# Inner normalisations of a hybrid decoder step: where the low parts of the new activations are made, and fewer throwaway products

## The chip, the cores and the metric

One core of one Trainium2 chip runs the whole program. The metric is the device time of one execution in microseconds (us); lower is better. Beside it there is one profiled execution with a trace of every engine: TensorE (PE, and PEld for its weight loads), VectorE (DVE), ScalarE (ACT), GpSimd (POOL) and the queue that loads weights (SP).

## The reference

One inference step of a two-layer decoder trunk for 288 token rows: 256 of a new sequence and 32 of eight running ones. Around each of the two mixers (first RWKV-7 beside retention, then gated DeltaNet) stand two SwiGLU networks. Every one of these six parts is followed by a normalisation:

```python
def layer_norm(x, g, b):
    xf = x.astype(jnp.float32)
    xc = xf - jnp.mean(xf, -1, keepdims=True)
    var = jnp.mean(xc * xc, -1, keepdims=True)
    return xc * lax.rsqrt(var + LN_EPS) * g + b
...
def trunk(x, pos0, states, p):
...
    for l in range(DEPTH):
        i = l // 2
        f = swiglu(h, p['ffn_w_gate'][l, 0], p['ffn_w_up'][l, 0], p['ffn_w_down'][l, 0])
        h = layer_norm(DEEPNORM_ALPHA * h + 0.5 * f, p['ln_g'][l, 0], p['ln_b'][l, 0])
...
        h = layer_norm(DEEPNORM_ALPHA * h + m, p['ln_g'][l, 1], p['ln_b'][l, 1])
        f = swiglu(h, p['ffn_w_gate'][l, 1], p['ffn_w_up'][l, 1], p['ffn_w_down'][l, 1])
        h = layer_norm(DEEPNORM_ALPHA * h + 0.5 * f, p['ln_g'][l, 2], p['ln_b'][l, 2])
```

All is computed in single precision.

## The kernel before, in words

**Layout.** The activations lie transposed: 1024 channels are eight tiles (d = 0 to 7) of 128 rows by 288 tokens. `r3` holds the residual sum, `x` the activations. For TensorE each operand is split in a high part, which a short format holds exactly, and the low part that is left: `xhi` and `xlo` for the activations, `whi` and `wlo` for the weights. A product is three matmuls in a row, high by high (L2265), high by low weight (L2266) and low by high weight (L2269).

**Weights** come in units of 128 output channels. In the stages that follow a normalisation a unit has eight tiles of 128x128, so 24 matmuls. SP loads the units into four buffers. ACT makes the high part of a unit (`split_hi`, L2223), DVE the low part (`split_lo`, L2228), each into one of two buffers; a unit is split as soon as the unit two before it has been used. On ACT and DVE the order of the work is written out: in an `up` stage they first deal with the result of the unit that is done (ACT the gate function, L2347; DVE the product with the gate, L2438) and then split the unit two ahead.

**Phases** run in the order ffn0, norm0, ab0, norm1, ffn1, norm2, ffn2, norm3, gdn0, norm4, ffn3, norm5. The first five normalisations are the inner ones. norm0 is followed by the stage `za` (whose ACT and DVE code is in `ab_scalar` and `ab_vector`), norm1, norm2 and norm4 by an `up` stage, norm3 by the one-unit stage `ba` and then `qk` of the DeltaNet mixer.

**A normalisation** is spread over four engines, each with its own function `norm` (on POOL `sum_tiles`):

- POOL adds the first seven tiles of `r3` while the stage before ends (L2524).
- PE multiplies that sum and the last tile with a matrix of 1/1024, which gives the mean (L2291, L2293); later the eight squares in the same way, which gives the variance (L2298). Then come `WARM` = 16 throwaway products into a bank that nobody reads (`keep_warm`, L2285; single precision, so each is two matmul records). Then the stage that follows begins; its first unit waits before each matmul for the tile of `xhi` or `xlo` that it reads (L2264, L2268).
- DVE subtracts the mean (L2462), splits a unit of weights, takes the reciprocal (L2471), and scales eight tiles of `r3` in place (L2473, semaphore `scaled`). After all eight it makes eight low parts: tile plus bias minus `xhi` (L2479, semaphore `x_lo`, one for even and one for odd tiles).
- ACT squares (L2365), splits a unit of weights, takes the root (L2370), and after each scaling makes a high part: tile plus bias, rounded (L2376, semaphore `x_hi`). After all eight it makes the eight whole tiles of `x` in full precision (L2381, semaphore `x_new`), which the next residual sum reads. It then loads the function table of the next stage (L2354 in an `up` stage, L1678 in `ba`).

At that time both units of weights that fit in the buffers are already split, so the third unit of the stage is the first to be split after the normalisation.

**POOL after a normalisation.** In norm0 it goes on at once to `ab_pool`: it issues a transfer of old rows (L1323), clears a column, and copies the rows into place (L1326, semaphore `shift_pad`), for which ACT waits before the first rows of `za`. After norm1 it issues the transfer of constants for the DeltaNet mixer. After norm3 it goes to `gdn_pool`: a transfer (L2088), and a copy (L2091, semaphore `conv_pad`), for which DVE waits after the stage `ba`, ahead of its short operations on the decay rows (from L1882). In the `up` stages it splits the hidden activations.

The helper `low_parts` (L390 to L393) makes low parts on DVE and POOL elsewhere, at the input and at the end of both mixers, by a plain subtraction.

Of the kernel before, what the change touches and what calls it, by code (L numbers as in the profile page):

```python
# [23 lines left out]
DT = D // P  # L24
# [37 lines left out]
WARM = 16  # L62
# [235 lines left out]
def delta_kernel(nc, a):  # L298

    ctx = ExitStack()  # L300
    with ctx:
# [2015 lines left out]
        def _(act):  # L2317
# [38 lines left out]
            def norm(n):  # L2356
# [9 lines left out]
                if second_unit(n):  # L2366
# [4 lines left out]
                                     bias=eps).then_inc(drained[bank_of(("var", n))], 1)  # L2371
                for d in range(DT):
                    act.wait_ge(sem("scaled"), DT * n + d + 1)
                    b = pc("ln_b", n * DT + d)
                    if f"norm{n}" != phases[-1]:
                        nc.scalar.activation(xhi[:, d, :], r3[:, d, :], ACT.Identity, bias=b).then_inc(x_hi, 1)  # L2376
                    else:
                        nc.scalar.activation(x[:, d, :], r3[:, d, :], ACT.Identity, bias=b).then_inc(sem("x_new"), 1)
                if f"norm{n}" != phases[-1]:
                    for d in range(DT):  # L2380
                        nc.scalar.activation(x[:, d, :], r3[:, d, :], ACT.Identity, bias=pc("ln_b", n * DT + d)  # L2381
                                             ).then_inc(sem("x_new"), 1)
# [25 lines left out]
        def _(dve):  # L2408
# [47 lines left out]
            def norm(n, stage_name):  # L2456
# [14 lines left out]
                link(nc.vector.reciprocal(m(T, T), m(0, T)))  # L2471
                for d in range(DT):
                    nc.vector.scalar_tensor_tensor(out=r3[:, d, :], in0=r3[:, d, :], scalar=pc("ln_g", n * DT + d),  # L2473
                                                   in1=m(T, T), op0=ALU.mult, op1=ALU.mult
                                                   ).then_inc(sem("scaled"), 1)
                if f"norm{n}" != phases[-1]:
                    for d in range(DT):
                        dve.wait_ge(x_hi, DT * X_VERSION[n] + d + 1)
                        nc.vector.scalar_tensor_tensor(out=xlo[:, d, :], in0=r3[:, d, :],  # L2479
                                                       scalar=pc("ln_b", n * DT + d),  # L2480
                                                       in1=xhi[:, d, :].bitcast(F32), op0=ALU.add,
                                                       op1=ALU.subtract).then_inc(x_lo[d % 2], 1)
# [23 lines left out]
        def _(pool):  # L2506
# [9 lines left out]
            def sum_tiles(n):  # L2516
# [10 lines left out]
                ins.then_inc(sem("summed"), 1)  # L2527

# [152 lines left out]
```

## Time and profile before

| what | us |
|---|---|
| median of three runs | 1718.11 |
| lowest and highest of them | 1716.66, 1719.91 |
| span of the profiled execution, first to last instruction | 1714.2 |
| PE busy in it | 1592.8 |
| DVE, ACT, POOL busy in it | 890.9, 644.6, 407.2 |
| mean granted clock of TensorE in it | 0.944 of full |

The span is the profiled execution's own time on the engines; no other time is listed for that execution, and the runs' times are taken around the program as a whole. A row of a timeline gives the start, the duration, the engine, the line, the operation, what it writes and reads, how many like it follow without a break (x8), and in brackets the idle time of the engine before it and what ended that. A matmul's duration includes its way through the array, so that records overlap; its cost in a stream is the step to the next start.

### The profile page before, as it was taken

To read this page: it belongs to the slowest core of one execution; us is meant where nothing else is said; L and a number is where in the kernel's file an instruction comes from. 1 tells how busy PE (TensorE), PEld (TensorE's weight loads), DVE (VectorE), ACT (ScalarE), POOL (GpSimd) and SP (SyncE) were. 2 spreads that over 40 slices of the span, in tenths; PEclk is the share of its full clock that TensorE was granted. 3 is DMA by queue.
4 is the path that set the end of the run, shared out by engine and by line. 5 is a ranking of instruction groups with operands and counts; after the bars stand their busy time and mean duration, and the time that the engine had idled before them with its cause. 6 is when DMAs were issued, how large, how long until landed. Compare 5 with 4: busy or idle time off the path is not lost.

```text
span 1714.2 us, 29766 instructions
## 1 busy us (share of the span) xinstructions
PE 1592.8 (93%) x11529; PEld 1498.7 (87%) x11529; DVE 890.9 (52%) x1235; ACT 644.6 (38%) x997; POOL 407.2 (24%) x442
## 2 busy tenths in 40 slices
PE   8999998798998799999999999898798987999997
PEld 7999987788788589999999999797785885899996
DVE  4444468754254364444544444786654734644444
ACT  4333365211032343333443333654634113533423
POOL 3332005324011322330023310000325413133200
PEclk9999999899599899999999999998998886999999
DMA  7555433000042145555345554242400201354551
GB/s 263 160 166 181 157 99 111 15 2 26 4 163 96 43 148 160 170 174 171 123 132 163 165 186 150 83 153 101 148 1 7 99 7 67 106 171 160 177 170 61
DMA packets 50614, 203.05 MB, mean 118 GB/s; under 512 B 5696, under 2 KB 5696, under 8 KB 49888
## 3 DMA queue, kind: packets, MB, share of 16 engines
q1 hardware_dynamic: 46224, 181.03, 32.1%
q0 software_dynamic: 4016, 19.61, 3.1%
q8 instruction: 63, 1.03, 0.2%
q10 hardware_dynamic: 288, 1.18, 0.2%
q14 instruction: 23, 0.19, 0.0%
HBM read 191.97 MB, written 9.83 MB: 118 GB/s over the span
## 4 chain that ended last, share of the span: by engine, by line
PE 81%; DVE 10%; ACT 4%; issue 3%; POOL 1%; DMA 0%; DVEq 0%; ACTq 0%; POOLq 0%
PE gemm L2265 20%; PE gemm L2269 19%; PE gemm L2266 19%; PE job L850 2%; PE gemm L2285 2%; DVE wlo L2228 2%; PE job L1551 2%; ACT whi L2223 1%; PE job L2298 1%; PE job L1662 1%; PE job L836 1%; PE job L1612 1%; PE job L1528 1%; PE job L662 1%; PE job L686 1%
## 5 line engine op out<-in xcount | busy, mean ns | idle before, releaser
L2228 DVE TENSOR_TENSOR wlo<-raw,whi 128x1024 fp32r<-128x1024 f32 (+1 forms) x319 | 424.0, 1329 | 468.4 <-ACT whi L2223 468.2
L2265 PE MATMUL gemm<-xhi,whi 128*128 128x288 f32 x2040 | 618.7, 303 | 29.4 <-DVE wlo L2228 19.4
L2269 PE MATMUL gemm<-xlo,whi 128*128 128x288 f32 x2040 | 606.9, 297 | 3.9 <-DVE xlo L392 3.8
L2266 PE MATMUL gemm<-xhi,wlo 128*128 128x288 f32 x2040 | 608.2, 298 | 0.0
L2223 ACT ACTIVATE whi<-raw 128x1024 fp32r<-128x1024 f32 (+1 forms) x319 | 358.0, 1122 | 486.7 <-PE gemm L2269 480.9
L2265 PEld LDWEIGHTS gemm<-xhi,whi 128*128 128x128 f32 x2040 | 389.0, 191 | 42.1 <-DVE wlo L2228 22.5
L2269 PEld LDWEIGHTS gemm<-xlo,whi 128*128 128x128 f32 x2040 | 390.2, 191 | 4.8 <-DVE xlo L392 4.1
L2266 PEld LDWEIGHTS gemm<-xhi,wlo 128*128 128x128 f32 x2040 | 389.6, 191 | 1.3
L2265 PE MATMUL gemm<-hhi,whi 128*128 128x288 f32 x704 | 208.5, 296 | 0.9 <-DVE wlo L2228 0.9
L2269 PE MATMUL gemm<-hlo,whi 128*128 128x288 f32 x704 | 208.7, 296 | 0.0
L2266 PE MATMUL gemm<-hhi,wlo 128*128 128x288 f32 x704 | 205.2, 292 | 0.0
L2537 POOL TENSOR_TENSOR hlo<-hb,hhi 128x288 f32 x88 | 140.3, 1595 | 14.4 <-POOL hhi L2535 14.4
L2535 POOL CAST hhi<-hb 128x288 f32 x88 | 37.4, 425 | 427.9 <-DVE hb L2438 427.9
L2266 PEld LDWEIGHTS gemm<-hhi,wlo 128*128 128x128 f32 x704 | 134.2, 191 | 0.0
L2265 PEld LDWEIGHTS gemm<-hhi,whi 128*128 128x128 f32 x704 | 132.2, 188 | 1.9 <-DVE wlo L2228 1.9
L2269 PEld LDWEIGHTS gemm<-hlo,whi 128*128 128x128 f32 x704 | 131.9, 187 | 0.0
L2347 ACT ACTIVATE sg<-gemm 128x288 f32<-128x288 f32 x88 | 36.2, 411 | 187.9 <-PE gemm L2269 187.9
L2438 DVE TENSOR_TENSOR hb<-sg,gemm 128x288 f32<-128x288 f32 x88 | 39.9, 454 | 54.1 <-PE gemm L2269 54.1
L2524 POOL TENSOR_TENSOR xsum<-xsum,r 128x288 f32<-128x288 f32 x30 | 26.0, 868 | 170.1 <-DVE r L2451 169.7
L1673 ACT ACTIVATE M<-job 128x512 f32<-128x512 f32 (+4 forms) x46 | 24.2, 530 | 105.3 <-PE job L1528 70.4
L2451 DVE SCALAR_TENSOR_TENSOR r<-x,gemm 128x288 f32 (+1 forms) x48 | 21.8, 454 | 75.3 <-PE gemm L2269 75.3
L861 ACT ACTIVATE M<-job 128x512 f32<-128x512 f32 (+6 forms) x44 | 18.6, 441 | 87.4 <-PE job L540 23.1
(405 smaller groups left out, 1781.8 us busy)
## 6 DMA issues: line engine op xcount, KB each, us to landing
raw<-in_w_dram SPq DMA_DIRECT2D x255, 512.0 KB, 3.3
raw<-in_w_dram SPq DMA_DIRECT2D x64, 704.0 KB, 4.0
s_space<-in_gdn_in_dram POOLq DMA_DIRECT2D x8, 512.0 KB, 6.3
out_gdn_s_dram<-s_space POOLq DMA_DIRECT2D x8, 512.0 KB, 3.0
M<-in_ret_in_dram POOLq DMA_DIRECT2D x1, 2048.0 KB, 9.1
out_ret_s_dram<-M POOLq DMA_DIRECT2D x1, 2048.0 KB, 8.1
x<-in_x_dram ACTq DMA_DIRECT2D x2, 576.0 KB, 6.5
out_y_dram<-x SPq DMA_DIRECT2D x2, 576.0 KB, 2.8
```

The costliest lines, as they stand in the source:

```text
L850: mm = pe.matmul(bank[:, h * P:(h + 1) * P], lhs[s][:, h, :], rhs[s][:, h, :], start=True, stop=True)
L1551: mm = pe.matmul(bank[:, h * P:(h + 1) * P], lhs[:, h, :], rhs[:, h, :], start=True, stop=True)
L2223: nc.scalar.activation(whi[c % SPL][:, 0:w], raw[c % RAW][:, 0:w], ACT.Copy).then_inc(hi_ready, 1)
L2228: nc.vector.tensor_tensor(wlo[c % SPL][:, 0:w], raw[c % RAW][:, 0:w], whi[c % SPL][:, 0:w].bitcast(F32), ALU.subtract).then_inc(lo_ready, 1)
L2265: pe.matmul(bank[:, 0:T], whi[s][:, w], hi[:, f0 + q, :], start=first, stop=False)
L2266: pe.matmul(bank[:, 0:T], wlo[s][:, w], hi[:, f0 + q, :], start=False, stop=False)
L2269: mm = pe.matmul(bank[:, 0:T], whi[s][:, w], lo[:, f0 + q, :], start=False, stop=last)
L2285: pe.matmul(gemm[0][:, 0:T], C("mean"), xsum[:], start=True, stop=True)
L2347: nc.scalar.activation(sg[:, j // 2, :], gemm[j][:, 0:T], ACT.Silu).then_inc(bank_free[j], 1)
L2438: nc.vector.tensor_tensor(hb[:, h, :], sg[:, h, :], gemm[j][:, 0:T], ALU.mult).then_inc(bank_free[j], 1)
L2535: nc.gpsimd.tensor_copy(hhi[:, f, :], hb[:, h, :]).then_inc(hid_hi, 1)
L2537: nc.gpsimd.tensor_tensor(hlo[:, f, :], hb[:, h, :], hhi[:, f, :].bitcast(F32), ALU.subtract).then_inc(hid_lo, 1)
```

## The change

Three edits, all at the five inner normalisations (the last one, whose result goes to the output, is left as it was).

1. On DVE the low part of tile d - 1 is made right after the scaling of each odd tile d, so that the order is: scale 0, scale 1, low 0, scale 2, scale 3, low 2, and so on. DVE makes no low parts of odd tiles.
2. ACT makes the whole tile of each odd d right after its high part, and the whole tiles of even d at the end. POOL makes the low part of each odd tile as the whole tile minus the high part, after its sum of tiles, waiting for `x_new`.
3. `WARM` is 10.

```diff
-WARM = 16
+WARM = 10
...
+                def whole(d):
+                    nc.scalar.activation(x[:, d, :], r3[:, d, :], ACT.Identity, bias=pc("ln_b", n * DT + d)
+                                         ).then_inc(sem("x_new"), 1)
+
                 for d in range(DT):
                     act.wait_ge(sem("scaled"), DT * n + d + 1)
-                    b = pc("ln_b", n * DT + d)
-                    if f"norm{n}" != phases[-1]:
-                        nc.scalar.activation(xhi[:, d, :], r3[:, d, :], ACT.Identity, bias=b).then_inc(x_hi, 1)
-                    else:
-                        nc.scalar.activation(x[:, d, :], r3[:, d, :], ACT.Identity, bias=b).then_inc(sem("x_new"), 1)
+                    if f"norm{n}" == phases[-1]:
+                        whole(d)
+                        continue
+                    nc.scalar.activation(xhi[:, d, :], r3[:, d, :], ACT.Identity, bias=pc("ln_b", n * DT + d)
+                                         ).then_inc(x_hi, 1)
+                    if d % 2 == 1:
+                        whole(d)
                 if f"norm{n}" != phases[-1]:
-                    for d in range(DT):
-                        nc.scalar.activation(x[:, d, :], r3[:, d, :], ACT.Identity, bias=pc("ln_b", n * DT + d)
-                                             ).then_inc(sem("x_new"), 1)
+                    for d in range(0, DT, 2):
+                        whole(d)
...
+                def low(d):
+                    dve.wait_ge(x_hi, DT * X_VERSION[n] + d + 1)
+                    nc.vector.scalar_tensor_tensor(out=xlo[:, d, :], in0=r3[:, d, :],
+                                                   scalar=pc("ln_b", n * DT + d),
+                                                   in1=xhi[:, d, :].bitcast(F32), op0=ALU.add,
+                                                   op1=ALU.subtract).then_inc(x_lo[0], 1)
+
                 for d in range(DT):
                     nc.vector.scalar_tensor_tensor(out=r3[:, d, :], in0=r3[:, d, :], scalar=pc("ln_g", n * DT + d),
                                                    in1=m(T, T), op0=ALU.mult, op1=ALU.mult
                                                    ).then_inc(sem("scaled"), 1)
-                if f"norm{n}" != phases[-1]:
-                    for d in range(DT):
-                        dve.wait_ge(x_hi, DT * X_VERSION[n] + d + 1)
-                        nc.vector.scalar_tensor_tensor(out=xlo[:, d, :], in0=r3[:, d, :],
-                                                       scalar=pc("ln_b", n * DT + d),
-                                                       in1=xhi[:, d, :].bitcast(F32), op0=ALU.add,
-                                                       op1=ALU.subtract).then_inc(x_lo[d % 2], 1)
+                    if d % 2 == 1 and f"norm{n}" != phases[-1]:
+                        low(d - 1)
...
                 ins.then_inc(sem("summed"), 1)
+                if f"norm{n}" != phases[-1]:
+                    for d in range(1, DT, 2):
+                        pool.wait_ge(sem("x_new"), DT * n + d // 2 + 1)
+                        nc.gpsimd.tensor_tensor(xlo[:, d, :], x[:, d, :], xhi[:, d, :].bitcast(F32), ALU.subtract
+                                                ).then_inc(x_lo[1], 1)
```

## Rows read from the trace of the kernel before

**Rows 1.** The page: the span, and the chain that ended last by engine.

```profile
span 1714.2 us, 29766 instructions
...
PE 81%; DVE 10%; ACT 4%; issue 3%; POOL 1%; DMA 0%; DVEq 0%; ACTq 0%; POOLq 0%
```

**Rows 2.** The timeline of DVE at norm1: start us, duration us, what.

```profile
628.25 3.52 DVE L2473 SCALAR_TENSOR_TENSOR r<-r,par,M 128x288 f32<-128x288 f32 x8
631.69 3.51 DVE L2479 SCALAR_TENSOR_TENSOR xlo<-r,par,xhi 128x288 fp32r<-128x288 f32 x8
638.55 1.22 DVE L2228 TENSOR_TENSOR wlo<-raw,whi 128x1024 fp32r<-128x1024 f32 x1 [3.35 <-ACT whi L2223]
```

**Rows 3.** The timeline of ACT at norm1.

```profile
628.80 3.54 ACT L2376 ACTIVATE xhi<-r,par 128x288 fp32r<-128x288 f32 x8 [2.57 <-DVE r L2473]
632.24 3.51 ACT L2381 ACTIVATE x<-r,par 128x288 f32<-128x288 f32 x8
635.77 1.28 ACT L2354 ACT_TABLE_LOAD   x1
...
637.46 1.05 ACT L2223 ACTIVATE whi<-raw 128x1024 fp32r<-128x1024 f32 x1
```

**Rows 4.** The timeline of PE at norm1: throwaway products, first unit, third unit.

```profile
625.52 7.92 PE L2285 MATMUL gemm<-xsum,cst 128*128 128x288 f32 x32
633.07 0.51 PE L2265 MATMUL gemm<-xhi,whi 128*128 128x288 f32 x1
633.42 0.29 PE L2266 MATMUL gemm<-xhi,wlo 128*128 128x288 f32 x1
...
639.83 0.40 PE L2265 MATMUL gemm<-xhi,whi 128*128 128x288 f32 x1
```

**Rows 5.** The timeline of ACT after norm0: the splits of two successive units.

```profile
240.45 1.06 ACT L2223 ACTIVATE whi<-raw 128x1024 fp32r<-128x1024 f32 x1 [0.97 <-PE gemm L2269]
...
243.65 1.06 ACT L2223 ACTIVATE whi<-raw 128x1024 fp32r<-128x1024 f32 x1 [1.78 <-PE gemm L2269]
```

**Rows 6.** The chain of waits after norm3, in order of time: start us, us, what.

```profile
1084.00 3.51 ACT x L2381 x8
...
1095.20 0.31 DVE mixc L1882
...
1099.36 0.40 PE gemm L2265
```

**Rows 7.** The view of line L392: ns shortest/median/longest, first and last start.

```profile
L392 POOL TENSOR_TENSOR xlo<-M,xhi x8: 792/1008/2439, 578.0 to 1447.4; 128x288 fp32r<-128x288 f32 x8
```

**Rows 8.** The timeline of POOL at the end of the first mixer.

```profile
578.01 0.88 POOL L392 TENSOR_TENSOR xlo<-M,xhi 128x288 fp32r<-128x288 f32 x1 [12.72 <-ACT xhi L995]
```

**Rows 9.** The timeline of DVE at the same time.

```profile
578.15 1.05 DVE L1286 SCALAR_TENSOR_TENSOR M<-M,par,r 128x288 f32<-128x288 f32 x1
```

**Rows 10.** The timeline of DVE at norm0.

```profile
231.97 3.53 DVE L2473 SCALAR_TENSOR_TENSOR r<-r,par,M 128x288 f32<-128x288 f32 x8
```

**Rows 11.** The timeline of POOL at norm0: the transfer and the copy after the sums.

```profile
215.45 0.57 POOL L1323 DMA_DIRECT2D M<-in_shift_in_dram  x1
...
217.52 0.39 POOL L1326 COPY M<-M 128x112 f32<-128x112 f32 x1 [1.36 <-DMA M<-in_shift_in_dram]
```

**Rows 12.** The timeline of POOL at norm3: the same two steps.

```profile
1071.85 0.57 POOL L2088 DMA_DIRECT2D M<-in_conv_in_dram  x1 [8.38 <-DVE r L2451]
...
1074.99 0.78 POOL L2091 COPY M<-M 128x576 f32<-128x576 f32 x1 [2.38 <-DMA M<-in_conv_in_dram]
```

**Rows 13.** Stretches: length, then PE, PEld, DVE, ACT, POOL busy; PEclk, DMA, GB/s.

```profile
369.50:372.90 3.40, 1.94 (x14) 1.62 (x14) 3.37 (x7) 0.00 (x0) 0.00 (x0) 1.00 0.00 0
372.90:376.30 3.40, 3.40 (x18) 3.40 (x18) 3.33 (x4) 0.77 (x2) 2.94 (x2) 0.51 0.00 0
...
495.80:499.20 3.40, 1.78 (x12) 1.32 (x10) 3.40 (x8) 1.06 (x1) 1.53 (x1) 1.00 0.90 371
499.20:502.60 3.40, 3.29 (x24) 3.29 (x25) 3.33 (x8) 0.00 (x0) 0.72 (x1) 1.00 0.52 174
```

## The prediction

> **What bounds the kernel now.** I read the page first, then the stretch around one inner normalisation on the three engines, then the chain of waits at the one normalisation that differs. The page shows TensorE on 81% of the chain that ended last, in a span of 1714.2 us [rows 1]. So an inner normalisation matters only through the moment at which PE can stream the weight units that follow it. The reader should see in norm1 that three engines work in rows: DVE scales eight tiles and then makes eight low parts [rows 2]; ACT makes eight high parts, then eight whole tiles, and only then loads the table for the next stage and splits the weights of the third unit [rows 3]; PE runs 16 throwaway products (32 records) from 625.52, starts the first unit at 633.07 and the third at 639.83 [rows 4].
>
> I count from the first scaling, 628.25 = 0. ACT ends its last whole tile at 632.24 + 3.51 = 635.75, which is 7.50. The third unit follows from that alone: table load, gate, high split (637.46 + 1.05), low split (638.55 + 1.22 = 639.77), PE at 639.83 [rows 2 to 4]. A unit of 24 products takes 3.20 us, the step between two high splits that each wait for one (240.45 to 243.65) [rows 5], so 0.133 us a product. The second unit therefore begins at 633.42 + 23 x 0.133 = 636.48 (8.23) and ends at 11.43; the third begins at 11.58, 0.15 us later, because ACT and DVE were the later ones [rows 4]. So **the tail of ACT, not the throwaway products, sets the third unit** after norm1, and norm2 and norm4 are followed by the same kind of stage. After norm3 the chain of waits runs through ACT's whole tiles (1084.00, 3.51 us) into DVE's short operations at 1095.20 and PE at 1099.36 [rows 6]: ACT again. Only after norm0 does PE's own first unit release ACT's next split (240.45, after 0.97 us idle for PE) [rows 5].
>
> **The change part by part.**
>
> *Six throwaway products fewer.* 7.92 us / 16 is about 0.49 us each [rows 4]; six are 2.9 us, so PE is free at about 2.1 instead of 4.8. It then waits for low parts, so this is worth nothing by itself; what covers it is the wait below.
>
> *The order of DVE and ACT.* The step from one scaling or high part to the next is 0.43 us ((631.69 - 628.25) / 8, and the same on ACT); one alone takes what eight in a row take less seven steps, 3.52 - 3.01 = 0.51 and on ACT 0.53 and 0.50, so 0.52; from DVE to ACT pass 0.04 (628.25 + 0.51 to 628.80) [rows 2, 3]. DVE now has four low parts in place of eight, which alone would end it 1.7 us sooner. But each low part stands between scalings and waits for a high part that waits for a scaling. A pair costs 0.51 + 0.04 + 0.52 + 0.04 + 0.43 = 1.54 us, where two scalings cost 0.86. The seventh scaling starts at 3 x 1.54 = 4.62, the eighth ends at 4.62 + 0.43 + 0.51 = 5.56, its high part starts at 5.60, and five whole tiles follow at steps of 0.43: the last ends at 5.60 + 5 x 0.43 + 0.52 = 8.27, or 8.28 with less rounding. ACT has the same sixteen operations as before, now with three stalls: **0.78 us later**, even if nothing else interferes.
>
> *Odd low parts on POOL.* Such a subtraction takes 0.79 us at the least and 2.44 at the most [rows 7]. While POOL held one (578.01, 0.88 us [rows 8]), the very form that DVE uses here, 128x288 with a per-partition scalar, took 1.05 instead of 0.51 us [rows 2, 9], so the later one waits for the other. In the new order POOL asks for tile 1 just after 1.94 (first whole tile), while DVE is at scaling 4 until 2.49; POOL then ends at about 3.14 and the low part of tile 2, ready at 2.65, ends at 3.45 instead of 3.17: +0.28. Tile 3 comes at about 3.57, falls into the fifth scaling, and holds the sixth until 4.85, which sets low part 4 back by 0.3. Tile 5 comes behind the eighth scaling, tile 7 when DVE is done (7.25 to 8.05). Sum +0.57: ACT ends at 8.85, **1.35 later than 7.50**. Bounds: 0.78 if POOL always finds a gap; if POOL gets in ahead of a scaling in each of the first pairs, two full delays of 0.54 and a little more, ACT ends at 9.5, +2.0. I take 1.35, since the row shows an operation already running to its end first.
>
> The Trainium skill states in "SBUF — State Buffer", section "SBUF: two separate sides", that a VectorE instruction with two SBUF inputs and a GpSimd one that reads SBUF exclude each other for the whole instruction, whichever starts first. By that rule every scaling and every low part counts, and the sum is the +5.4 below. The longest POOL row, 2.44 us, is longer than one instruction of waiting would make it; if POOL always waited so long for a pause of DVE, the sum would lie nearer to +2.6.
>
> *The first unit.* Its last product needs tile 7 from POOL at 8.05, so the second unit starts at about 8.25: as before (8.23). Bounds: 7.66 without the interference (-0.56), 8.87 with the worst (+0.65). I take 0. It counts at norm0 alone, since elsewhere ACT is later.
>
> *What POOL issues later.* The four subtractions stand ahead of what POOL did early. At norm0 the first scaling stands at 231.97 [rows 10], so POOL is done at 240.0. The shift transfer (215.45) and its copy 2.07 us later [rows 11] move to there, the copy to 242.1 to 242.5. ACT's first rows wait for that; its next split is due at 243.65 [rows 5], and 0.6 us of rows fit, so nothing; cover gone, each microsecond more of the transfer is one on PE. After norm3, whose first scaling is at 1084.00 - 3.99 = 1080.0 [rows 2, 3, 6], transfer and copy (1071.85 to 1075.77) [rows 12] move to about 1088 and 1092, before DVE needs them at 1095.20 [rows 6]: nothing. After norm1 the constants for a stage 450 us away: nothing.
>
> *Sum.* norm1, norm2, norm4: third unit +1.35 each. norm3: +1.35 through the chain of [rows 6]. norm0: 0. Together +5.4 us; bounds 4 x 0.78 - 0.56 = +2.6 and 4 x 2.0 + 0.65 = +8.7. The profiled execution's span is 1714.2; the median of the runs is 1718.11, 3.9 us more, and no other time of that execution is listed; I add the sum to the median, taking what lies around the span as unchanged. 1718.1 + 5.4 = **1723.5**, +0.31%.
>
> **The rivals.**
>
> *POOL and DVE don't get in each other's way* (not slower, by the measure below). The subtractions fall into DVE's three waits for high parts, about 0.25 us each. For: the gaps exist. Against: POOL needs 0.8 us, and the 1.05 us row. Only the order costs: 4 x 0.78 - 0.56 = +2.6, **1720.7**. It decides if no scaling in the changed trace takes over 0.6 us. Chance 0.20.
>
> *The low parts do set the units* (faster side). If the third unit's splits had room, each of five first units would end 0.56 sooner: -2.8, **1715.3**. It decides where ACT's last whole tile ends before 7.5, or its later work can slip. Against it, the 0.15 us by which ACT and DVE are already late at 639.83 [rows 2, 4]. Chance 0.10, half of it below the measure.
>
> *PE's clock falls.* With fewer throwaway products PE waits inside the first unit: between 4.6 and 8.0 it has some 12 products, 1.6 us of work. Elsewhere in the trace a stretch with 1.94 of 3.40 us busy was followed by 0.51, the lower level of 1.2 GHz, and one with 1.78 of 3.40 us was followed by 1.00 [rows 13], so either may come. Half clock for 3.4 us loses 1.7 us; after norm1, norm2 and norm4 the 1.4 us in which PE waits for the third unit take most of that, after norm0 nothing does. One such stretch at each adds 1.7 + 4 x 0.3 = 2.9 (at norm3 taken like the three); a second one at each is no longer covered and makes it 3.4 + 4 x 2.0 = 11.4. At the lower third of that, +5 on top of the forecast: **1728.5**. Chance 0.20.
>
> **How the numbers follow.** The forecast (1720.7 to 1726.8 by its bounds) has 0.50. A measurement of this kernel can tell about 0.2%, 3.4 us, from no change. Slower by more than that: forecast and clock, 0.70. Within: no interference 0.20 and half of the faster rival, 0.25. Faster: the other half, 0.05. The range takes in the forecast's bounds, the case without interference, and the nearer half of the clock's: 1719 to 1730; left out are the faster rival, 0.1, and the worse half of the clock's, 0.1. The forecast's own range is 1720.7 to 1726.8.
>
> **What would show it.** ACT's last whole tile should end 8.3 to 9.5 us after the first scaling (7.50 before); scalings or low parts of about 0.8 to 1.05 us beside POOL's subtractions; PE's third unit after norm1, norm2 and norm4 with about 1.3 us of idle before it, waiting for the low split; after norm3 PE's restart (1099.36) 1.35 us later against the scalings; after norm0 no change. The prediction is wrong if the third unit starts no later against the first scaling than 11.58, or if the granted clock drops behind a normalisation.

## The result, and the profile after

The changed kernel takes 1721.89 us in the median of 20 executions (1717.91 to 1734.28), the kernel before 1717.11 in 20 of the same series (1711.08 to 1722.06). The ratio is **1.0039, 95% interval 1.0025 to 1.0052**: slower by +4.8 us between the medians, where +5.4 was forecast. The ratio is not the quotient of the two medians (that is 1.0028); by the ratio the change costs 6.7 us (4.3 to 8.9). Five of the 20 lie above 1729, where none of the kernel before does (of its 109 executions in the later series one does, at 1731.12).

The page of the kernel after, its span and the chain that ended last, as in [rows 1]:

```profile
span 1717.8 us, 29646 instructions
...
PE 77%; DVE 12%; ACT 6%; issue 3%; POOL 1%; DMA 1%; DVEq 0%; ACTq 0%; POOLq 0%
```

PE has 4 points less of the chain than before, DVE and ACT have them. The timeline of DVE at norm1 of the kernel after (start us, duration us, what, and in brackets the idle time ahead with what ended it); the first scaling, 631.30, is 0, and [rows 2] are the same stretch before:

```profile
631.30 0.95 DVE L2485 SCALAR_TENSOR_TENSOR r<-r,par,M 128x288 f32<-128x288 f32 x2
632.42 0.52 DVE L2479 SCALAR_TENSOR_TENSOR xlo<-r,par,xhi 128x288 fp32r<-128x288 f32 x1 [0.18 <-ACT xhi L2381]
632.86 0.94 DVE L2485 SCALAR_TENSOR_TENSOR r<-r,par,M 128x288 f32<-128x288 f32 x2
633.98 0.80 DVE L2479 SCALAR_TENSOR_TENSOR xlo<-r,par,xhi 128x288 fp32r<-128x288 f32 x1 [0.17 <-ACT xhi L2381]
634.70 1.48 DVE L2485 SCALAR_TENSOR_TENSOR r<-r,par,M 128x288 f32<-128x288 f32 x2
636.11 0.51 DVE L2479 SCALAR_TENSOR_TENSOR xlo<-r,par,xhi 128x288 fp32r<-128x288 f32 x1
636.54 0.93 DVE L2485 SCALAR_TENSOR_TENSOR r<-r,par,M 128x288 f32<-128x288 f32 x2
637.64 0.80 DVE L2479 SCALAR_TENSOR_TENSOR xlo<-r,par,xhi 128x288 fp32r<-128x288 f32 x1 [0.17 <-ACT xhi L2381]
```

The timeline of POOL in the same stretch:

```profile
633.32 1.14 POOL L2538 TENSOR_TENSOR xlo<-x,xhi 128x288 fp32r<-128x288 f32 x1 [11.26 <-ACT x L2373]
634.88 1.00 POOL L2538 TENSOR_TENSOR xlo<-x,xhi 128x288 fp32r<-128x288 f32 x1 [0.41 <-ACT x L2373]
637.26 0.86 POOL L2538 TENSOR_TENSOR xlo<-x,xhi 128x288 fp32r<-128x288 f32 x1 [1.39 <-ACT x L2373]
638.54 0.81 POOL L2538 TENSOR_TENSOR xlo<-x,xhi 128x288 fp32r<-128x288 f32 x1 [0.42 <-ACT x L2373]
```

A low part takes 0.52 us when DVE is alone and 0.80 where it begins while POOL subtracts (633.98, inside 633.32 + 1.14). The pair of scalings at 634.70 takes 1.48 in place of 0.95: the sixth scaling alone takes 1.05, beside POOL's subtraction of tile 3. The timeline of ACT and then that of PE, which answer to [rows 3, 4]:

```profile
637.95 2.23 ACT L2373 ACTIVATE x<-r,par 128x288 f32<-128x288 f32 x5
640.19 1.28 ACT L2354 ACT_TABLE_LOAD   x1
...
641.89 2.21 ACT L2223 ACTIVATE whi<-raw 128x1024 fp32r<-128x1024 f32 x2
```

```profile
638.18 0.40 PE L2269 MATMUL gemm<-xlo,whi 128*128 128x288 f32 x1 [0.83 <-POOL xlo L2538]
...
639.64 0.29 PE L2265 MATMUL gemm<-xhi,whi 128*128 128x288 f32 x1
...
644.25 0.40 PE L2265 MATMUL gemm<-xhi,whi 128*128 128x288 f32 x1 [1.25 <-DVE wlo L2228]
```

ACT's last whole tile ends at 640.18, 8.87 after the first scaling (7.50 before). The second unit starts at 8.34 (8.23 before), the third at 12.95 (11.58 before), after 1.25 us in which PE waits for the low split. After norm2 and norm4 the same times come out within 0.02 us. After norm3 the chain of waits of the kernel after runs as in [rows 6]; from the first scaling (1085.84) to PE's restart it is 20.72 us, where it was 1099.36 - 1080.00 = 19.36:

```profile
1092.49 2.18 ACT x L2373 x5
...
1102.40 0.31 DVE mixc L1882
...
1106.56 0.40 PE gemm L2265
```

**Where the time is over the whole program** is read from stretches that run from the first scaling of one normalisation to that of the next. For the kernel after (length, busy time of PE, PEld, DVE, ACT and POOL, granted clock, DMA share, GB/s): first mixer, two SwiGLU stretches, second mixer, third SwiGLU stretch.

```profile
231.79:631.30 399.51, 352.28 (x2690) 312.65 (x2689) 219.76 (x350) 122.16 (x209) 109.58 (x108) 0.87 0.20 68
631.30:858.47 227.17, 222.64 (x1626) 218.25 (x1625) 105.30 (x111) 88.90 (x111) 53.23 (x55) 1.00 0.47 155
858.47:1085.84 227.37, 222.83 (x1626) 218.27 (x1625) 105.30 (x112) 88.89 (x111) 52.69 (x54) 1.00 0.47 152
1085.84:1483.36 397.52, 348.58 (x2307) 308.23 (x2306) 246.74 (x422) 168.64 (x343) 100.04 (x128) 0.88 0.23 79
1483.36:1710.53 227.17, 220.06 (x1614) 215.91 (x1612) 102.88 (x110) 86.90 (x109) 52.72 (x54) 1.00 0.43 140
```

The same view of the kernel before:

```profile
231.97:628.25 396.28, 350.12 (x2702) 311.74 (x2701) 219.89 (x355) 121.72 (x209) 105.75 (x101) 0.88 0.21 70
628.25:854.04 225.79, 224.20 (x1638) 220.37 (x1637) 106.07 (x115) 88.59 (x111) 48.83 (x50) 1.00 0.47 154
854.04:1080.00 225.96, 224.37 (x1638) 220.35 (x1637) 105.82 (x115) 88.59 (x111) 50.31 (x53) 1.00 0.47 155
1080.00:1481.11 401.11, 350.37 (x2319) 309.16 (x2318) 247.08 (x426) 167.76 (x343) 94.50 (x121) 0.89 0.23 78
1481.11:1706.91 225.80, 221.65 (x1626) 218.03 (x1624) 103.39 (x114) 86.57 (x109) 48.84 (x50) 1.00 0.43 141
```

The three SwiGLU stretches are 1.38, 1.41 and 1.37 us longer: the late third unit, no more and no less. The mixers differ by +3.2 and -3.6 us, and of these stretches they alone have a clock below 1.00, in both kernels. So the profile supports the terms of norm1, norm2 and norm4, and leaves open what the mixers do. The experiments go after both.

### The profile page after: what moved, and what is told of

Its sections match the earlier page's. It is cut to its first block, busy times and chain, and to the rows that moved or that the text cites. A ratio compares the mean times of both kernels' runs of the same rounds, so it can differ in the third digit from the quotient of the medians.

```text
span 1717.8 us, 29646 instructions
## 1 busy us (share of the span) xinstructions
PE 1588.5 (92%) x11469; PEld 1492.3 (87%) x11469; DVE 888.6 (52%) x1215; ACT 646.8 (38%) x997; POOL 426.0 (25%) x462
## 4 chain that ended last, share of the span: by engine, by line
PE 77%; DVE 12%; ACT 6%; issue 3%; POOL 1%; DMA 1%; DVEq 0%; ACTq 0%; POOLq 0%
PE gemm L2265 19%; PE gemm L2269 19%; PE gemm L2266 18%; DVE wlo L2228 2%; PE job L850 2%; ACT whi L2223 2%; PE job L1551 2%; PE job L836 1%; PE job L2298 1%; PE job L1662 1%; PE job L1612 1%; PE job L1528 1%; DVE M L1860 1%; ACT x L2373 1%; PE job L662 1%
## 5 line engine op out<-in xcount | busy, mean ns | idle before, releaser
L2269 PE MATMUL gemm<-xlo,whi 128*128 128x288 f32 x2040 | 609.7, 299 | 12.2 <-POOL xlo L2538 7.9
```

What stands on the lines that cost most here:

```text
L2269: mm = pe.matmul(bank[:, 0:T], whi[s][:, w], lo[:, f0 + q, :], start=False, stop=last)
```

## The experiments

Each execution lists its span and its mean granted clock. The granted clock takes two levels in these traces, 1.00 and 0.50 of full (2.4 and 1.2 GHz), so the time at the lower one is 2 x (1 - clock) x span; for the profiled execution after it gives 2 x 0.06 x 1717.8 = 206 us (205.1 from its rows). The clock has three digits, so one value is good to 1.7 us, a mean of ten to less. In the table, "half" is the mean of this time over a series, the ratio is to the kernel before in the same series, "SwiGLU" the stretch after norm1 and "second mixer" the stretch after norm3, both in the profiled execution.

| kernel | n | median us | ratio to before (95%) | half, us | SwiGLU | second mixer |
|---|---|---|---|---|---|---|
| before (in the series of the first four experiments) | 24 | 1718.98 | | 203.0 | 225.8 | 401.1 |
| after | 20 | 1721.89 | 1.0039 (1.0025 to 1.0052) | 217.7 | 227.2 | 397.5 |
| e1, after with 16 products | 12 | 1721.12 | 1.0019 (1.0006 to 1.0032) | 205.5 | 227.2 | 397.5 |
| e2, before with 10 products | 12 | 1717.93 | 1.0009 (0.9987 to 1.003) | 212.5 | 225.8 | 398.1 |
| e3, no POOL, 10 products | 6 | 1732.53 | 1.0086 (1.0061 to 1.011) | 227.4 | 228.0 | 405.7 |
| e4, DVE not interleaved | 7 | 1726.18 | 1.0044 (1.0027 to 1.0062) | 219.2 | 225.8 | 404.5 |
| e5, before with a longer tail | 12 | 1718.62 | 1.0005 (0.9988 to 1.0021) | 200.4 | 227.2 | 397.7 |
| e6, POOL only writes | 12 | 1719.25 | 1.0009 (0.9988 to 1.0031) | 208.3 | 228.1 | 400.7 |
| e7, whole tiles on POOL | 12 | 1717.77 | 0.9977 (0.9955 to 0.9999) | 208.2 | 224.6 | 410.4 |
| e8, no POOL, 16 products | 10 | 1726.58 | 1.0055 (1.0031 to 1.0079) | 215.3 | 226.7 | 398.3 |
| e9, after again | 10 | 1724.62 | 1.0053 (1.003 to 1.0077) | 219.1 | 227.2 | 411.9 |
| e10, e5 again | 12 | 1721.08 | 1.0016 (1.0002 to 1.003) | 203.7 | 227.2 | 397.5 |
| e11, before again | 8 | 1717.78 | 0.9989 (0.9966 to 1.0011) | 195.8 | 225.8 | 401.2 |
| e12, e7 again | 12 | 1719.72 | 0.9995 (0.9971 to 1.0019) | 214.2 | 224.6 | 410.5 |

**e1: the new order with 16 throwaway products** (edit of the kernel after).

```diff
-WARM = 10
+WARM = 16
```

> The changed kernel with 16 throwaway products in place of 10. Theory: the order of DVE, ACT and POOL alone costs the time, because ACT's last whole tile ends 8.87 us after the first scaling in place of 7.50. Then nothing changes here against the changed kernel: ACT's tail at 8.87, the third unit after norm1, norm2 and norm4 at 12.95, the time 4 to 6 us above the kernel before. Rival, the clock: the loss comes from PE's waits with too few throwaway products; then the time comes back to within 2 us of the kernel before, and no half clock is granted behind norm3.

ACT's tail ends at 8.87, the second unit starts at 8.35 and the third at 12.94, all as in the kernel after; PE no longer waits inside the first unit. So the six products are free in this place, as the prediction had it. The total is 2.1 us above before by the medians and 3.3 by the ratio (1.0 to 5.5), where 4 to 6 were expected; nor does the rival hold, for behind norm3 the clock is still low for 6.8 us. Yet the time at half clock is 205.5 us in place of 217.7, no execution lies above 1726, and the mean span is 1719.4 where that of the kernel after is 1722.5.

**e2: the old order with 10 products** (edit of the kernel before).

```diff
-WARM = 16
+WARM = 10
```

> The kernel before with 10 throwaway products and nothing else. Theory: PE is free at 1.9 us after the first scaling and then waits for the low parts of DVE, the last of which ends at 6.95; the second unit starts at about 7.2 in place of 8.23, but the third unit stays at 11.58 after norm1, norm2 and norm4, held by ACT's tail. Only norm0 gains, about 1 us: 0.5 to 1.5 us faster than the kernel before. Rival, the clock: slower than before by 2 to 10 us, with half clock granted behind one or more of the normalisations.

PE waits 1.45 us for the first low part, the second unit starts at 7.25 (8.23 before) and the third after norm1, norm2 and norm4 at 11.58, unchanged: there ACT sets it. Only norm0's third unit gains (10.45 for 11.42). The total is inconclusive, and the half clock went up to 212.5: two of the twelve executions, at 1729.8 and 1729.9, have 242 us of it each. In the profiled one the rival's half clock shows behind norm3 alone, for 3.4 us.

**e3: odd low parts on DVE, behind the even ones, nothing on POOL** (edit of the kernel after).

```diff
                 if f"norm{n}" != phases[-1]:
-                    for d in range(1, DT, 2):
-                        pool.wait_ge(sem("x_new"), DT * n + d // 2 + 1)
-                        nc.gpsimd.tensor_tensor(xlo[:, d, :], x[:, d, :], xhi[:, d, :].bitcast(F32), ALU.subtract
-                                                ).then_inc(x_lo[1], 1)
...
+                    for d in range(1, DT, 2):
+                        low(d)
```

> The changed kernel, but DVE makes the odd low parts too, after its last interleaved one, and POOL makes none. Theory: only the loop of scaling, high part and low part is left, 1.54 us a pair; no scaling or low part takes over 0.6 us, ACT's last whole tile ends at 8.28, the third unit after norm1, norm2 and norm4 starts at 12.36, after norm3 PE restarts 0.78 later than before; the time is 2.5 to 4 us above the kernel before, 2 to 3 us below the changed one. Rival, POOL's later transfers hold the mixers: back to the kernel before within 1 us.

No scaling takes over 0.52 us and the tail ends at 8.30, both as expected. The total missed by far. PE's timeline has a wait of 3.83 us for tile 1, and the stretch behind it shows the lower clock level, as do those behind all five inner normalisations:

```profile
639.52 0.61 PE L2269 MATMUL gemm<-xlo,whi 128*128 128x288 f32 x1 [3.83 <-DVE xlo L2479]
...
639.00:642.40 3.40, 2.88 (x12) 2.89 (x13) 1.75 (x5) 3.37 (x7) 0.00 (x0) 0.50 0.00 0
```

Here the SwiGLU stretches carry it: 2.2 to 2.5 us longer than before, where the tail alone would make 0.8. The third unit after norm1, norm2 and norm4 starts at 13.88 to 14.13 (12.36 expected) and waits for nothing: PE's own first unit, held for tile 1 and at half clock behind that, now sets it. So this run does not test the tail; e6 does.

**e4: DVE scales all eight tiles first, then makes the four even low parts** (edit of the kernel after).

```diff
-                    if d % 2 == 1 and f"norm{n}" != phases[-1]:
-                        low(d - 1)
+                if f"norm{n}" != phases[-1]:
+                    for d in range(0, DT, 2):
+                        low(d)
```

> The changed kernel, but DVE scales all eight tiles first and makes its four low parts afterwards; POOL makes the odd ones, ACT's order and 10 throwaway products as in the changed kernel. Theory: ACT never waits for DVE, its last whole tile ends at 7.5 again and the third unit after norm1, norm2 and norm4 starts at 11.6, although scalings beside POOL's subtractions take 0.8 to 1.05 us; the second unit starts at about 7.2; the time is 0 to 2 us below the kernel before. Rival, the shared access of DVE and POOL is the main cost: ACT's tail stays over 8.3 and the time 3 us or more above the kernel before.

The interference is still there (DVE's timeline: eight scalings in 4.61 us in place of 3.52, and low parts of 1.05), but ACT, which has high parts and whole tiles to make meanwhile, does not wait for it: the tail ends at 7.48, and the SwiGLU stretches after norm1 and norm2 are those of before.

```profile
628.86 4.61 DVE L2485 SCALAR_TENSOR_TENSOR r<-r,par,M 128x288 f32<-128x288 f32 x8
633.39 2.89 DVE L2479 SCALAR_TENSOR_TENSOR xlo<-r,par,xhi 128x288 fp32r<-128x288 f32 x4
```

The order on DVE is thus what lets the tail become late. The total missed: PE waited 2.54 us inside the first unit, the clock fell behind norm0, norm3 and norm4, and the ratio is 1.0044.

**e5: only a longer tail** (edit of the kernel before: ACT writes three whole tiles once more).

```diff
+                    act.wait_ge(sem("x_new"), DT * (n + 1))
+                    for d in range(3):
+                        nc.scalar.activation(x[:, d, :], r3[:, d, :], ACT.Identity, bias=pc("ln_b", n * DT + d))
```

> The kernel before (old order, 16 throwaway products, nothing on POOL) with three whole tiles written a second time by ACT at each inner normalisation, after a wait for its own eighth. Theory: ACT's tail alone sets the third unit. The last whole tile ends at about 8.8 to 8.9 after the first scaling, as in the changed kernel; the third unit after norm1, norm2 and norm4 starts at 12.9 to 13.0 though PE's first unit is as before (second unit at 8.23); from norm1 to norm2 and from norm2 to norm3 each takes 1.3 to 1.5 us longer; the time is 3 to 7 us above the kernel before. Rival, that PE's waits in the first unit or POOL make the loss: the time stays within 1.5 us of the kernel before.

ACT's and then PE's timeline at norm1 (first scaling 632.50): the three tiles add 1.4 us, the third unit starts at 12.99 and waits 1.39.

```profile
640.04 1.39 ACT L2385 ACTIVATE x<-r,par 128x288 f32<-128x288 f32 x3
...
645.49 0.40 PE L2265 MATMUL gemm<-xhi,whi 128*128 128x288 f32 x1 [1.39 <-DVE wlo L2228]
```

All three SwiGLU stretches are 1.26 to 1.42 us longer, +4.1 together, but the ratio is 1.0005: the total missed. In this profiled execution the second mixer took 397.7 us, 3.4 less than before, and the first 401.5, 5.3 more, so that its span is 4.9 us above that of the profile before.

**e6: POOL writes zeros and reads nothing** (edit of the kernel after).

```diff
-                        nc.gpsimd.tensor_tensor(xlo[:, d, :], x[:, d, :], xhi[:, d, :].bitcast(F32), ALU.subtract
-                                                ).then_inc(x_lo[1], 1)
+                        nc.gpsimd.memset(xlo[:, d, :].bitcast(F32), 0.0).then_inc(x_lo[1], 1)
```

> The changed kernel, but POOL writes zeros into the odd low parts in place of subtracting; so the low parts of odd tiles are left out of the result. It reads nothing there. Theory: what made scalings and low parts longer was POOL's reading beside DVE; now none takes over 0.6 us, ACT's last whole tile ends at 8.28, the third unit after norm1, norm2 and norm4 starts at 12.36, and the time is 2 to 3 us below the changed kernel, 2 to 4 above the kernel before. Rival, that any work of POOL holds DVE: scalings of 0.8 us and more stay and ACT's tail stays over 8.6.

POOL's and then DVE's timeline at norm1 (first scaling 627.77): POOL's write at 632.87 lies within DVE's scalings at 632.43, and DVE keeps its times.

```profile
632.87 0.34 POOL L2538 MEMSET xlo<- 128x288 f32 x1 [1.21 <-ACT x L2373]
```

```profile
632.43 0.94 DVE L2485 SCALAR_TENSOR_TENSOR r<-r,par,M 128x288 f32<-128x288 f32 x2
633.54 0.52 DVE L2479 SCALAR_TENSOR_TENSOR xlo<-r,par,xhi 128x288 fp32r<-128x288 f32 x1 [0.18 <-ACT xhi L2381]
```

The tail ends at 8.30 and the third unit starts at 12.38. So of the 1.37 us by which the tail moved, **0.80 belong to the order and 8.87 - 8.30 = 0.57 to the two engines getting in each other's way**. The Trainium skill ("SBUF — State Buffer", section "SBUF: two separate sides") says that a VectorE operation with two SBUF inputs (outside its two-port modes) is shut out only by a GpSimd operation that reads SBUF; with the subtraction DVE takes up to 1.05 us and with the write 0.52, so this trace agrees. The total is inconclusive, 1.0009; the 228.1 us after norm1 hold 3.4 us at half clock, and the other two stretches are 226.8 and 226.6.

**e7: another way to shorten the tail** (edit of the kernel before: after norm1 to norm4 POOL makes the whole tiles, and ACT goes on at once; 13 products).

```diff
-WARM = 16
+WARM = 13
...
+            def wholes(n):
+                for e in range(2):
+                    pool.wait_ge(x_lo[e], DT // 2 * (X_VERSION[n] + 1))
+                for d in range(DT):
+                    nc.gpsimd.tensor_scalar(x[:, d, :], r3[:, d, :], pc("ln_b", n * DT + d), None, ALU.add
+                                            ).then_inc(sem("x_new"), 1)
...
-                if f"norm{n}" != phases[-1]:
+                if n == 0:
```

> A version that should beat both: the order of the kernel before on DVE and for ACT's high parts, 13 throwaway products, but the whole tiles after norm1 to norm4 are made by POOL (tile plus bias), once all low parts are done, and ACT makes none there; after norm3 POOL does so behind its copy, and DVE waits for them before it uses the room of the residual again. Theory: with ACT's tail gone the low parts set the start: second unit at 7.2 to 7.3 and third unit at 10.4 to 10.5 (before 11.58) after norm1, norm2 and norm4, from normalisation to normalisation 1.1 us less; PE's restart after norm3 1.2 to 1.4 us earlier; the time 4 to 7 us below the kernel before. Rival, the tail is not what sets the third unit: no more than 1.5 us below.

The second unit starts at 7.25 and the third at 10.45 with no wait, PE's restart after norm3 comes 1.2 us earlier, and the SwiGLU stretches are 1.2 to 1.3 us shorter than before. The total gained 0.3 us by the medians and 4.0 by the ratio (0.2 to 7.7), where 4 to 7 were expected; the second mixer took 410.4 us in the profile, 9.3 more than before.

**e8: e3 with 16 products.**

```diff
-WARM = 10
+WARM = 16
```

> The kernel after with the odd low parts on DVE behind the even ones (as in the run without POOL) and 16 throwaway products in place of 10. Each execution lists its span and mean granted clock; 2 x (1 - mean clock) x span is its time at half clock: mean 203 us for the kernel before (24 executions), 205.5 for the new order with 16 products, 217.7 for the kernel after, 227.4 for the run without POOL with 10. Theory (the wait of PE behind the throwaway products brings the half clock, and six products more cover it): the wait for tile 1's low part shrinks from 3.83 to about 0.9 us, the granted clock stays at 1.00 behind the normalisations, time at half clock 202 to 210 us; ACT's tail still 8.30 and the third unit 12.38, so about +0.8 at each of four normalisations: median 1719.5 to 1723, against 1732.5 with 10. Rival A (the half clock comes from the first unit's uneven pace, whatever the products): it still falls behind the five normalisations, 220 us or more, median 1728 to 1733. Rival B (the half clock is gone but was not what the time went to): no fall, and still over 1727.

PE's timeline: the wait for tile 1 shrinks to 0.92 us, and the clock stays at 1.00 behind every normalisation. The SwiGLU stretches are 226.7 to 227.0, 0.9 to 1.0 longer than before. That is not the tail of 8.30: the second unit starts at 9.41 (first scaling 634.60; 8.23 before), because the odd low parts come last, and the third one unit later at 12.61, without a wait, where the tail would have allowed 12.38. Start of the first product for tile 1, of the second and of the third unit:

```profile
641.38 0.40 PE L2269 MATMUL gemm<-xlo,whi 128*128 128x288 f32 x1 [0.92 <-DVE xlo L2479]
...
644.01 0.30 PE L2265 MATMUL gemm<-xhi,whi 128*128 128x288 f32 x1
...
647.21 0.30 PE L2265 MATMUL gemm<-xhi,whi 128*128 128x288 f32 x1
```

Of the theory this holds: six products cover those falls. But the median, 1726.58, is above the 1719.5 to 1723 expected, and the mean time at half clock is 215.3 us; the profiled execution has 208.0, all of it in the mixers but for 6.6 us at the end. Two of the ten executions lie at 1734 with 232 us, so 16 products do not keep a kernel from such executions. The falls behind the normalisations were only part of what the time went to.

**e9: the kernel after again**, without an edit.

> The kernel after once more, unchanged, for its spread. Theory (ten products leave the granted clock on an edge): mean time at half clock 212 to 222 us where the kernel before on this chip has 199 to 207; median 1720 to 1724; 2 to 7 of 12 executions above 1726, each with over 225 us at half clock. Rival (the upper group belonged to that one series): none above 1726, time at half clock as before, median about 1720.

Four of ten executions lie above 1726, each with 224.9 to 232.1 us at half clock, as expected; the median is 0.6 us above what was expected. The profiled execution is one of the four, 1730.0 us in place of 1717.8, so it shows where those 12.2 us lie. The same stretches as above:

```profile
231.05:629.03 397.98, 352.02 (x2690) 313.61 (x2689) 218.55 (x350) 122.22 (x209) 109.54 (x108) 0.88 0.20 68
629.03:856.20 227.17, 224.03 (x1626) 219.65 (x1625) 105.53 (x111) 88.94 (x111) 53.16 (x55) 0.99 0.48 155
856.20:1083.60 227.40, 222.86 (x1626) 218.30 (x1625) 105.34 (x111) 88.92 (x111) 52.68 (x54) 1.00 0.47 153
1083.60:1495.52 411.92, 361.85 (x2307) 316.98 (x2306) 247.73 (x421) 168.69 (x343) 99.56 (x128) 0.85 0.23 76
```

The second mixer alone is 14.4 us longer, with its clock at 0.85 in place of 0.88; the rest agrees, the first mixer being 1.5 us shorter. Behind norm1 the clock was low for 3.4 us (0.99), and the stretch is 227.17 all the same: PE's wait for the third unit took that up.

**e10: e5 again**, without an edit.

> The kernel before with ACT's three whole tiles written again, once more, for its spread: the SwiGLU stretches were 1.41 us longer each, the total only 0.5 us above before (-2.1 to +3.6). Theory (each late third unit counts in full): median 2 to 5 us above before, at a like time at half clock (198 to 206 us). Rival (something in the mixers gives it back): again within 1.5 us of before, with SwiGLU stretches of 227.2.

SwiGLU stretches of 227.22 again; the ratio is 1.0016 (+2.8 us, interval +0.3 to +5.2). With e5 (+0.9, interval -2.1 to +3.6) the tail alone is worth about 2 us, less than the 4.1 of the stretches. By the median (+1.0) it is the rival that holds, by the interval neither falls.

**e11: the kernel before again**, without an edit.

> The kernel before once more, for a second profiled execution. Theory (the mixers' lengths differ from one execution to the next by their time at half clock, the SwiGLU stretches don't): SwiGLU stretches 225.8 to 226.0 again, within 0.2; mixers anywhere between 392 and 405 us. Rival: the mixers come out at 396.3 and 401.1 within 1 us, so that their lengths belong to a kernel and differences between kernels there have causes in the kernel.

The SwiGLU stretches come out within 0.1 us of the first profile. The first mixer is 399.1 us in place of 396.3, and the second 401.2, as before: the theory held for the one, the rival for the other. The first mixer had 105.8 us at half clock in place of 92.2, the second 92.2 both times.

**e12: e7 again**, without an edit.

> The kernel with the whole tiles on POOL and 13 throwaway products once more: 0.9977 of before [0.9955, 0.9999] in the first series. Theory (the SwiGLU stretches are 1.2 us shorter in every execution and the mixers no longer on average): stretches 224.6, median 2 to 7 us below the kernel before of the same series. Rival (the first series was lucky in the mixers): within 2 us of before, or above it.

The ratio is 0.9995 (0.9971 to 1.0019): the rival holds. POOL's timeline shows what replaced ACT's tail, eight whole tiles in a row, 1.28 us each on average, off the path:

```profile
638.19 10.28 POOL L2535 TENSOR_SCALAR x<-r,par 128x288 f32<-128x288 f32 x8 [16.38 <-DVE xlo L2481]
```

The stretches are 1.2 us shorter again, and the second mixer took 410.5 us, as in e7. No version here is shown to beat the kernel before.

**What a mixer loses at half clock** can be seen in one piece of the second mixer, found by counting instructions back from norm4, so that it holds the same 135 matmuls in both kernels. In the profile of the kernel before, and then of the kernel after:

```profile
1391.33:1413.47 22.14, 19.71 (x135) 18.82 (x133) 5.02 (x15) 1.10 (x3) 5.46 (x20) 0.69 0.03 13
```

```profile
1401.01:1417.07 16.06, 13.63 (x135) 12.90 (x133) 5.01 (x15) 1.10 (x3) 5.48 (x20) 1.00 0.05 17
```

The other engines do the same work in the same time, and PE takes 6.1 us more where its clock was 0.69.

By the clock's records the second mixer was at half clock for 92.2 us in both profiles. But in the kernel after 10.2 of them lie behind norm3 before PE's restart, while the chain runs over ACT and DVE. From the restart to the first scaling of norm4 the profiles of before, after and e9 give

```profile
1099.36:1481.11 381.75, 335.36 (x2225) 295.69 (x2226) 234.95 (x401) 149.26 (x310) 94.50 (x121) 0.88 0.23 79
```

```profile
1106.56:1483.36 376.80, 331.97 (x2225) 293.59 (x2226) 234.94 (x401) 152.34 (x314) 94.73 (x121) 0.89 0.24 80
```

```profile
1104.32:1495.52 391.20, 345.78 (x2225) 302.97 (x2226) 235.94 (x400) 152.28 (x314) 94.25 (x121) 0.86 0.23 78
```

These are the same 2225 matmuls, with 92.2, 81.9 and 112.6 us at half clock. Of the kernel after against before, +1.36 at the restart and -4.95 behind it make the -3.59 of the second mixer. All fourteen profiles go this way: 376.7 to 376.9 us at 81.9 (after, e1, e5, e10), 381.8 at 92.2 (before, e11), 392.3 at 116.1 (e7, e12). A straight line through them has 0.46 us of length for each us at half clock; e3 lies 1.2 us off it, every other one 0.6 or less. So the second mixer's length follows the time that PE spends at half clock while it sets the pace.

## Why the prediction was right, and where not

**The total.** Slower by more than 0.2% was forecast with a chance of 0.70, and 1721.89 lies in the range, 1.6 us below the point. Part of that agreement may be two errors against each other, as the points on the products and on the sum tell.

**The order of DVE and ACT, +0.78.** Right: with POOL's reads gone (e6) the tail moves from 7.50 to 8.30.

**Odd low parts on POOL, +0.57.** Right to the hundredth, and in the places named: tile 1 ends at 3.16 (3.14 predicted), the low part of tile 2 at 3.47 (3.45), the sixth scaling at 4.88 (4.85), tile 7 runs from 7.24 to 8.05. Not foreseen was that the low part of tile 6 takes 0.80, beside the subtraction of tile 5, which starts before the eighth scaling ends and not behind it; ACT does not wait for that. The rival without interference falls with the 1.05 us scaling.

**The first unit, 0.** Right for the second unit: 8.34 for 8.23. But norm0 was costed at nothing, and its third unit starts at 243.56 - 231.79 = 11.77, before 11.42. The step named PE's own unit as what releases ACT's split there [rows 5]; the tail of 8.86 overtook it, and the split follows the whole tiles with no wait, as the timeline of ACT shows. Missed by 0.35 us.

```profile
240.56 1.05 ACT L2223 ACTIVATE whi<-raw 128x1024 fp32r<-128x1024 f32 x1
```

**POOL's later transfers, 0.** Right. At norm0 the copy ends at 242.25 and ACT's rows wait 0.67 us for it, but then ACT waits 0.82 for PE, as the same timeline shows further on; after norm3 the copy ends at 1097.72 and DVE needs it at 1102.40.

```profile
242.28 0.39 ACT L869 ACTIVATE M<-gemm 128x256 f32<-128x256 f32 x1 [0.67 <-POOL M L1326]
...
243.58 1.06 ACT L2223 ACTIVATE whi<-raw 128x1024 fp32r<-128x1024 f32 x1 [0.82 <-PE gemm L2269]
```

**Six products fewer, worth 0.** Right in the place (e1: the same third unit), doubtful for the program. Three pairs differ in nothing but the products, and each time 10 in place of 16 comes with more time at half clock: 212.5 against 203.0 (e2 and before), 217.7 against 205.5 (after and e1), 227.4 against 215.3 (e3 and e8). The mean spans go 1.2, 3.1 and 6.7 us the same way. The profiles of the third pair show where: e3 has five falls of 3.4 us behind the normalisations and e8 none, and the mixers of both hold 201.4 us without them. In the second pair the profiles of after and e1 have the same 105.8 us in the first mixer and the same 81.9 behind the restart in the second, so there the difference of the means lies in executions like that of e9. Between the kernel after and e1 it is 3.1 of the 5.7 us by which the mean span of the kernel after (1722.5) exceeds that of before (1716.8, in the series of e1); the kernel after was run in another series.

**The clock as a rival.** It was put behind the normalisations. There it is seen in e3 at all five and in e4 at three, with waits inside the first unit of 3.83 and 2.54 us; with 0.83 us, in the kernel after, it fell at none of norm0, norm1, norm2 and norm4 in one profile and at norm1 in the other, where it cost nothing, as the rival's working had it. The prediction also named a fall behind a normalisation as a sign that it is wrong, and by its letter that sign came: behind norm3 the clock fell in the kernel after, where it stayed at 1.00 up to PE's restart in the kernel before. But the chain ran over ACT and DVE meanwhile, so that the restart came no later than the tail makes it:

```profile
1092.90:1103.10 10.20, 7.78 (x32) 7.46 (x33) 1.97 (x4) 9.23 (x15) 2.30 (x4) 0.50 0.25 80
```

What the rival did not see is the mixers, where the execution of e9 lost its time.

**The sum, 4 x 1.35 into the median.** The terms were right where they arise: +1.37 to +1.41 at norm1, norm2 and norm4, +1.36 at PE's restart after norm3. The step that does not hold is taking them one to one into the total, with the rest as unchanged. A tail alone, +4.1 us in the three stretches and +1.4 at the restart, measured +0.9 and +2.8 by the ratios (e5, e10; the intervals end at +3.6 and +5.2). A gain of 3.7 us in the stretches and 1.2 at the restart measured -4.0 and -0.9 (e7, e12), but that kernel also gives POOL new work in the second mixer, which took 9.3 and 9.4 us more than before in its profiles. Where a tail is given back can be read in the second mixer: with the restart 1.4 us later, the profiles of after, e1, e5 and e10 have 81.9 us at half clock behind it and take 4.9 to 5.1 us less from there than that of before. It is not always so, for e9, the same kernel as after, has 112.6. By the ratios the tail costs 3.3 us with 16 products (e1, 1.0 to 5.5) and 6.7 with ten (4.3 to 8.9). So the forecast's +5.4 was probably too much for the tail and took nothing for the clock, but both intervals hold it, and that the two errors cancel is argued and not shown.

**What stays open.** What decides how much of a mixer passes at half clock was not tried. That throwaway products at a normalisation change it is suggested, and not shown, by series of 6 to 24 executions, in one direction three times. Within a series the time at half clock scatters by 7 to 14 us from one execution to the next, and the unchanged kernel before gave means of 203.0 to 204.6 in four series and 195.8 in e11.

## What to carry to other kernels

A loop of "produce, wait, consume" between two engines cost the sum of both steps in each turn here (1.54 us a pair in place of 0.86); interleaving can pay only where the engine that feeds the later tail does not have to wait for it. Price a tail in the place where it arises, but before adding it to the median, take a second profile of the unchanged kernel and see how far its other stretches move by themselves. Count the time at half clock only where PE sets the pace, and over many executions: throwaway products that are free on the path may still be worth something to the clock.

## What was not expected of the hardware

The second mixer came back to within 0.1 us in pairs of profiles: 401.11 and 401.17 (before, e11), 410.43 and 410.47 (e7, e12), and 397.52 twice in kernels that differ only in the products (after, e1). But two executions of one kernel gave 397.52 and 411.92 (after, e9). Behind PE's restart these had 92.2, 116.1, 81.9 and 112.6 us at half clock. The time at half clock of the whole stretch hides this: 92.2 us of it went with 401.11 in one kernel and 397.52 in another.
